# Moving operands walked from the last column to the first, in the feed-forward layers and the expert loop

## The reference

```python
# a feed-forward layer, d_ff = 2816, four times
def swiglu(h, w_gate, w_up, w_down):
    return (jax.nn.silu(h @ w_gate) * (h @ w_up)) @ w_down

# the experts: top 16 x 16 keys per head, 8 heads
act = jax.nn.gelu(jnp.einsum('thkd,td->thk', expert_u[ib], hb), approximate=False)
return jnp.einsum('thk,thkd->td', gb * act, expert_v[ib])
```

## Time and profile before

| | |
|---|---|
| median of 3 runs | 2041.28 us (2040.92 to 2041.61) |
| span of the profiled execution, first to last instruction | 2039.6 us |
| PE busy | 2005.6 us, 13232 matmuls |
| DVE busy | 1508.3 us |
| ACT busy | 1123.1 us |
| mean granted clock of TensorE | 0.998 of full speed |

### The profile page before, as it was taken

One profiled execution on the slowest core, in us unless ns is written; L12 is line 12 of the kernel. 1 busy time (PEld: TensorE's weight loads), 2 busy tenths in 40 slices (PEclk: granted clock), 3 DMA queues, 4 the chain that ended last, 5 costly groups with the idle time before them and its releaser, 6 DMA issues.

```text
span 2039.6 us, 37233 instructions
## 1 busy us (share of the span) xinstructions
PE 2005.6 (98%) x13232; PEld 1822.9 (89%) x13232; DVE 1508.3 (74%) x2564; ACT 1123.1 (55%) x1835; POOL 59.9 (3%) x40
## 2 busy tenths in 40 slices
PE   7999999999999999999999999999999999999998
PEld 6999999988888888888888999999999999999998
DVE  5868898877777777777777667776667667957666
ACT  5445537965555555555555555755555555655554
POOL 0000430000000000000000000000000000000000
PEclk9999999999999999999999999999999999999999
DMA  6445543055565666655665555455555555445553
GB/s 214 135 135 190 205 142 104 24 174 187 189 192 192 187 189 192 191 189 187 206 231 173 187 186 174 135 169 188 187 186 178 185 185 186 156 143 177 185 188 111
DMA packets 101466, 353.73 MB, mean 173 GB/s; under 512 B 11392, under 2 KB 16640, under 8 KB 101120
## 3 DMA queue, kind: packets, MB, share of 16 engines
q1 hardware_dynamic: 100944, 350.13, 52.5%
q10 hardware_dynamic: 432, 2.36, 0.3%
HBM read 348.77 MB, written 3.67 MB: 173 GB/s over the span
## 4 chain that ended last, share of the span: by engine, by line
PE 90%; DVE 7%; ACT 2%; issue 1%; DMA 0%; SPq 0%; DVEq 0%; ACTq 0%
PE front L2030 38%; PE acc L2030 35%; PE tile L2030 16%; DVE w_lo L1219 2%; ACT w_hi L715 1%; DVE rstd L1241 1%; ACT h_parts L741 0%; DMA raw<-stream 0%; PE front L2587 0%; DVE cand L1688 0%; DVE h_parts L1248 0%; DVE sq L1230 0%; DVE conv L1573 0%; DVE rest L1657 0%; DVE top_i L1653 0%
## 5 line engine op out<-in xcount | busy, mean ns | idle before, releaser
L1219 DVE TENSOR_TENSOR w_lo<-raw,w_hi 128x1024 fp32r<-128x1024 f32 x612 | 747.0, 1223 | 85.4 <-ACT w_hi L715 84.9
L715 ACT CAST w_hi<-raw 128x1024 fp32r<-128x1024 f32 x628 | 654.3, 1044 | 137.6 <-PE tile L2030 60.8
L2030 PE MATMUL front<-h_parts,w_hi 128*128 128x512 f32 (+1 forms) x2432 | 586.4, 377 | 4.2 <-ACT h_parts L741 2.5
L2030 PEld LDWEIGHTS front<-h_parts,w_hi 128*128 128x128 f32 x2432 | 436.5, 189 | 80.2 <-issue 2.4
L2030 PE MATMUL front<-h_parts,w_lo 128*128 128x256 f32 x2272 | 337.2, 282 | 0.0
L2030 PEld LDWEIGHTS front<-h_parts,w_lo 128*128 128x128 f32 x2272 | 318.8, 190 | 20.6
L2030 PE MATMUL tile<-h_parts,w_hi 128*128 128x256 f32 x1344 | 247.8, 286 | 5.1 <-DVE w_lo L1219 2.6
L2030 PEld LDWEIGHTS tile<-h_parts,w_hi 128*128 128x128 f32 x1344 | 209.5, 192 | 8.2 <-issue 4.9
L1304 DVE TENSOR_TENSOR scaled<-front,scaled 128x512 f32<-128x512 f32 x76 | 52.6, 692 | 215.1 <-ACT scaled L779 215.1
L2030 PE MATMUL acc<-w_hi,mid_hi 128*128 128x512 f32 x512 | 200.9, 392 | 2.1 <-DVE mid_lo L1793 1.7
L783 ACT ACTIVATE scaled<-scaled 128x256 f32<-128x256 f32 x188 | 78.6, 418 | 223.4 <-DVE scaled L1307 116.6
(11 more groups left out here) (324 smaller groups left out, 2519.5 us busy)
## 6 DMA issues: line engine op xcount, KB each, us to landing
raw<-stream SPq DMA_DIRECT2D x632, 512.0 KB, 3.7
early_u<-stream SPq DMA_DIRECT2D x20, 512.0 KB, 3.6
early_activations<-early_out SPq DMA_DIRECT2D x20, 128.0 KB, 3.5
scaled<-early_activations SPq DMA_DIRECT2D x10, 128.0 KB, 4.0
x<-x_t SPq DMA_DIRECT2D x2, 512.0 KB, 5.3
keysT<-keys_t ACTq DMA_DIRECT2D x1, 1024.0 KB, 6.3
attc<-attention_constants ACTq DMA_DIRECT2D x1, 1024.0 KB, 7.1
out_t<-h SPq DMA_DIRECT2D x4, 256.0 KB, 2.4
```

Of the source, the lines that this page charges most:

```text
L715: nc.scalar.copy(w_hi[:, s, :], raw[:, s, :]).then_inc(hi_ready, 1)
L1219: nc.vector.tensor_tensor(w_lo[:, s, :], raw[:, s, :], w_hi[:, s, :].bitcast(F32), ALU.subtract).then_inc(lo_ready, 1)
L2030: return nc.tensor.matmul(out, lhsT, rhs, start=start, stop=stop, **kw)
```

## The change

In `wide`, in the expert drain and in the feed-forward drain the moving operand is given with its columns in descending order, and the output as well, so that each result lands where it did before. In `wide` the two runs of 256 stay in their order, and each is reversed within itself. Other matmuls (the projections, the mixers, the products by `three` in `feed` and by `first_two`) stay as they are.

```diff
             def wide(bank, slot):
 
+                halves = bank.rearrange("p (a t) -> p a t", a=2)[:, :, ::-1]
                 for k in range(KT):
-                    mm(bank, w_hi[:, slot, k * P:(k + 1) * P], h_parts[:, :, k, :], k == 0, False,
+                    mm(halves, w_hi[:, slot, k * P:(k + 1) * P], h_parts[:, :, k, ::-1], k == 0, False,
                        skip_group_check=True)
                 for k in range(KT):
-                    ins = mm(bank[:, 0:T], w_lo[:, slot, k * P:(k + 1) * P], h_hi[:, k, :], False, k == KT - 1,
-                             skip_group_check=True)
+                    ins = mm(halves[:, 0, :], w_lo[:, slot, k * P:(k + 1) * P], h_hi[:, k, ::-1], False,
+                             k == KT - 1, skip_group_check=True)
                 return ins
...
                         a, c = [part[:, s % 2, b // 2 * P:(b // 2 + 1) * P] for part in (mid_hi, mid_lo)]
-                        hi, lo = [part[:, n % RING, b % 2 * D // 2:(b % 2 + 1) * D // 2] for part in (w_hi, w_lo)]
-                        mm(banks[:, b, :], a, hi, False, False, skip_group_check=True)
-                        mm(banks[:, b, :], c, hi, False, False, skip_group_check=True)
-                        ins = mm(banks[:, b, :], a, lo, False, False, skip_group_check=True)
+                        hi, lo = [part[:, n % RING, b % 2 * D // 2:(b % 2 + 1) * D // 2][:, ::-1]
+                                  for part in (w_hi, w_lo)]
+                        o = banks[:, b, ::-1]
+                        mm(o, a, hi, False, False, skip_group_check=True)
+                        mm(o, c, hi, False, False, skip_group_check=True)
+                        ins = mm(o, a, lo, False, False, skip_group_check=True)
...
-                        ins = three(acc[:, m, :], n % RING, m * P, mid_hi[:, s % 2, :], mid_lo[:, s % 2, :],
+                        ins = three(acc[:, m, ::-1], n % RING, m * P, mid_hi[:, s % 2, ::-1], mid_lo[:, s % 2, ::-1],
                                     begin and m % 2 == 0, False, skip_group_check=True)
```

## The result

The changed kernel takes 2053.5 us (2053.32 to 2053.57, 3 runs) against 2041.28 us: the ratio is 1.0059, with a 95% interval of 1.0041 to 1.0077. It is slower, by 12 us. The span of the profiled execution is 2051.7 us against 2039.6, its granted clock 0.997 against 0.998.

A forecast was written before the change was run, and what follows sets the result against it. The prediction took PE, never idle in the expert loop, as the bound: time is matmul count times start-to-start distance. Downward walks were priced at 0 us, so the median stays 2041.3 us, with a range of 2032 to 2140 us.

The forecast's parts named there:

- the likeliest case, no price: Reversed matmuls on PE: walking downwards costs 0 us, leaving 2041.3 us, itself 2037 to 2045; chance 65%.
- The 1330 us that hang on how the array is fed: The 7872 touched matmuls on PE: 1250 us for columns plus 83 us of fixed part, out of the 2039.6 us span.
- The sign of being wrong that it names: PE timeline after: prediction wrong if untouched `tile<-h_parts,w_hi` stays at 0.12 us spacing and the touched matmuls do not.
- the first two of these rows: Wide products' moving read of two runs 2048 columns apart, and DVE's gapped SBUF walk at line 1505: both cost nothing.
- About 0.010 us for each matmul whatever its length: PE spacing from two lengths: 0.424 ns a column plus this fixed part, 83 us over 7872 matmuls.
- The rival of a fixed price: Each downward matmul on PE pays about 0.010 us more: 83 us, 2124 us in all; chance 11%.
- The rival of a shrinking fixed part: Touched matmuls on PE lose fixed time, at most 83 us, down to 1958 us; chance 5%.
- Nothing in the trace speaks for it: Against a shrinking fixed part: eight wide products take 1.82 us in the expert loop and 1.84 in a feed-forward layer.
- The halved rate: Downward walks on PE lose pairing, two steps a column: 1250 us more, 3291 us; chance 16% with prices nearer the gaps'.
- the rule of the Trainium skill on 16-byte lines: SBUF reads: accesses staying in one 16-byte line run at full bandwidth, so a backward walk of 4-byte elements costs 0 us.

The follow-up runs named there:

- e11: Probe kernel without the model, place 0: moving operand read in blocks of 4, 16 or 64 columns, one group behind different groups; descending 4-column blocks 0.1183 us, 64-column blocks 0.120.
- e1: Changed kernel with outputs ascending again, only the moving operands reversed, so columns land mirrored; 2053.65 us, ratio 1.0059.
- e2: Changed kernel with moving operands ascending again, only the outputs reversed, so columns land mirrored; 2041.45 us, ratio 1.0.
- e6: Probe kernel without the model: weights, then moving operand, shifted in steps of 16 columns, both directions; 114.0 to 120.0 ns for 256 columns, 226.9 to 236.7 for 512.
- e7: Kernel before, all walks upwards, with w_hi and w_lo 64 bytes later and all behind them 256 bytes later; 2020.47 us, ratio 0.9896.
- e3: Kernel before with only the 256-column matmuls reversed (low weights by h_hi in the wide product, feed-forward drain); 2030.41 us, ratio 0.9945.
- e5: Probe kernel without the model, other engines idle: direction, operand shifts, lengths and element types varied; 0.1198 up, 0.1183 down for 256 columns, 0.2269 and 0.2335 for 512.
- e9: Kernel before with mid_hi and mid_lo 48 columns further and w_lo 16 columns later, all walks upwards; 2037.55 us, ratio 0.9979.
- e10: Kernel before with mid_hi and mid_lo 48 columns further and only the wide product's low-weight products with h_hi reversed; 2033.58 us, ratio 0.9962.

## Why the prediction was right and wrong

The time lies in the range, 2032 to 2140 us, and slower had a chance of 30%; but the likeliest case, no price, was wrong. That the range holds is partly luck: it was made for one price with the same sign for both lengths, and what came is a sum of gains and losses that its width happened to cover. With the short matmuls alone reversed the time is 2030.4 us, below it.

- What bounds the kernel was read rightly: the changed kernel is still PE from end to end, and all 12 us are distances between matmuls. The 1330 us that hang on how the array is fed made a price of 3% on 3648 of them count.
- The sign of being wrong that it names came: the untouched products `tile<-h_parts,w_hi` stayed at 120 ns, the touched ones moved to 233.3 and 118.3. The step that failed is "It is nearest to the first two of these rows, whose price is nothing, and I take nothing." Neither row could tell. The wide product's broken read jumps 2048 columns, a multiple of 64, and lands at the same place modulo 256 bytes, where by e11 a jump is free. The mixer's gaps are DVE's. The price is +6.6 ns for 512 columns and -1.7 ns for 256 (e1 and e2: it is the read), less 27 ns for each slow start that goes. In the feed-forward layers this sums to nothing (8.467 us before and after), in the expert layer to 100 ns a step.
- "About 0.010 us for each matmul whatever its length" was wrong in size and as a picture. The mean of eight short ones, 0.119, took in two quick starts of 113 and 119 ns; the steady distances give 0.417 ns for a column and 13.3 ns beside it. In bf16 the difference between the two lengths (0.2160 - 0.1094)/256 is 0.416 ns a column, too, one tick of 2.4 GHz. At that rate 256 columns need 106.7 ns and 512 need 213.3; the rest was 13.3 ns for both lengths before, by coincidence of place. In e6 it lies between 7 and 13 ns for 256 columns and between 13 and 23 for 512. With the straight line through two points I took for fixed what e7 changed by moving a buffer.
- The rival of a fixed price (11%, 2124 us) was right that a price falls on each matmul and that it is small, but wrong in its size and in having one sign for both lengths. The rival of a shrinking fixed part (5%) is what happens to the short matmuls; alone, in e3, it makes the kernel 11 us faster. "Nothing in the trace speaks for it" was not so: the mixer's products with `y_hi` and `y_lo` were 116 to 118 ns apart in the trace of before (medians by form), those with `h_parts` 120, with the same shape, and 1.84 against 1.82 us for eight wide products was a slow start.
- The halved rate did not come. By the rule of the Trainium skill on 16-byte lines (SBUF — State Buffer, "SBUF: two separate sides") the walk should have been free; e11 agrees within a line (reversal inside 16 bytes, 0 ns) and disagrees on the order of lines, 0.1183 against 0.1198 and 0.2333 against 0.2269.

What is shown: the read of the moving operand pays, the weights' place matters as much as its own, other engines do not matter, and in bf16 and plain f32, at the one place tried, direction is free. That the two reads of SBUF, of the weights to come and of the moving columns, get in each other's way is the cause that I infer and no run isolates; for it speaks that moving either operand gives nearly the same set of distances (e6). The Trainium skill (TensorE: Matmul & The Clock Gate, "Step-by-step: what each phase is for") has them on two independent ports, and says that loading weights steals nothing from a running matmul; line 129 of e5 against line 99, where the weights lie 64 bytes further, 0.1138 against 0.1198 (or 0.1179, as in e11), is hard to square with that. Why a given pair of places gives its number, and what state carries over from one group to the next, stays open.

## What to carry to other kernels

On an engine that is never idle, look at the distance between starts for each form to the nanosecond, and compare it with columns over clock; a remainder that differs between equal shapes at other addresses is worth a sweep of buffer offsets within 256 bytes before any reordering. Here one such offset (e7) gave 1.0%, more than any choice of direction that was tried (e3, 0.55%). Measure the whole sequence, since neighbours change each other's spacing (e9, e10), and split a change by form: this one hid an 11 us gain behind a 19 us loss (the two do not add up to 12 us, since neighbours differ).

## What the runs showed of the hardware

- fp32r matmuls of 256 columns upwards run every 113 to 123 ns, and those of 512 every 227 to 235 ns, depending on where weights and moving operand begin, modulo 256 bytes; bf16 109 and 216 ns in either direction (one place tried).
- At place 0 a read in descending 16-byte pieces costs +6.6 ns for 512 columns and -1.7 ns for 256; one that descends inside 64 bytes, with ascending 64-byte blocks, costs +40 and +13 ns.
- The direction of PSUM writes is free (2041.45 against 2041.41 us).
- The same stream of 256-column matmuls can settle at 113.3 or at 117.8 ns, according to the group before it.
